# Who makes the low halves of the gate weights: VectorE takes over half 0 in the state-space stage of a two-block transformer kernel

## The chip, the cores and the metric

The kernel runs on one core of a Trainium2 chip. The metric is the device time of one execution in microseconds (us). Engines are named as the profile names them: PE (TensorE, the matrix multiplies), PEld (its weight loads), DVE (VectorE), ACT (ScalarE), POOL (GpSimd) and SP (SyncE, which here only issues the weight transfers).

## The reference

The program computes two blocks of two layers each over 256 positions of 1024 channels. The second block (`second_block`) has in each layer a mixer with a sparse attention and a state-space branch, then a gated feed-forward network. The change touches the state-space scan of that mixer, which runs twice, once in each layer:

```
L = exp(where(tril, A_cs[l] - A_cs[s], -inf))      # per head, 32 heads in 4 groups of 8
y = (C B^T * L) @ (x * dt)  + x * d_skip           # CB is shared by the 8 heads of a group
y = y * silu(z)                                    # the gate product
```

Beside it PE computes `h @ w_in` for the two gates of the mixer (`g_attn`, `g_ssd`), which needs 1024 x 2048 weights.

## The kernel before

All matrix products with weights go through slabs. A slab holds 1024 x 256 weights in two halves of 128 x 1024 numbers (128 partitions, 8 chunks of 128). SP loads a half into `w_raw`; ACT rounds it to `w_hi` (L1157, a type that PE multiplies at full rate); then DVE or POOL makes the remainder `w_lo = w_raw - w_hi` (L477, `split_lo`). PE multiplies each chunk three times (L675 to L677: high by high, low by high, high by low), 48 matmuls to a slab. `w_raw`, `w_hi` and `w_lo` have three buffers each. A remainder is made two slabs ahead of its use (`SPLIT_AHEAD`), a rounding three ahead. Each engine's program is written out by hand, and the engines wait for each other by semaphores. `s.w_lo[half]` counts the remainders of each half; when another engine goes on with a half, it first waits until the earlier owner's last remainder is counted (`take_over`).

The state-space stage works on pairs of heads, 16 pairs `c` to a layer, in groups of four that share one `cbm`. In this text "pair" always means a pair of heads. For each pair:

- PE writes the running sums of both heads into `logit` (L1088), and DVE takes differences of them (L2096, four instructions, `ssd_seg`).
- ACT takes the exponential of each head (L1530).
- DVE multiplies by `cbm` (L2104, 128x768, `ssd_m`), and PE multiplies by the inputs (L1122, eight matmuls into `tr` or `stat`).
- DVE adds the skip term (L2112, `ssd_out`, for the pair before), and POOL multiplies by the gate (L644, `ssd_gate`).

At the start of a group PE makes the group's `CB` (L1106, L1108) and DVE masks it (L2117, L2118). PE runs one slab of the gate weights ("gates") ahead of the products of every even pair. ACT rounds a later slab as soon as a slab is done, and after every odd slab it also takes one or two sigmoids (L1523), for which it loads another table and then the table of the exponential again. After the 16th pair DVE makes the last gate product itself (L2136), ACT squares (L1537), POOL adds the squares (L657), and DVE norms the groups (L2152, L2155, L486) beside the slabs of stage "pa"; the slabs of "ps" need the normed values.

Once in every two pairs, after an odd pair, DVE makes half 1 of the slab that is two ahead (`weights`, L1607 to L1610) right behind L2112, and POOL makes half 0 behind the gate products of the two pairs before. A gate product of an even pair and DVE's remainder wait for the same L2112, or follow it. Where this text says "inner piece" it means DVE's remainder behind the second pair of a group, and "end piece" the one behind the fourth, just ahead of the next L2117.

Of the kernel before, what the change touches and what calls it, by code (L numbers as in the profile page):

```python
# [19 lines left out]
ROUND_AHEAD, SPLIT_AHEAD = 3, 2  # L20
# [171 lines left out]
def build(nc, dram):  # L192
    ctx = ExitStack()
    with ctx:
# [269 lines left out]
        def slabs(stage, body, l=None):  # L464
            for n in range(COUNT[stage]):
                body(slab_at(stage, n, l), n, n % RING)
# [62 lines left out]
        @block.gpsimd  # L529
        def _(pool):  # L530
            def norm_lo(n, chunks):

                hi, lo = norm_set(n)
                for c in chunks:
                    pool.wait_ge(s.h_hi, DC * n + c + 1)
                    pool.wait_ge(s.h_f32, DC * n + c + 1)
                    lo_part(pool, lo[:, c, :], gained(n)[:, c, :], hi[:, c, :]).then_inc(s.h_lo_p, 1)

            def scaled_lo(layer):

                hi, lo = scaled_set(layer)
                for c in range(DC // 2):
                    pool.wait_ge(s.n_hi, DC * layer + c + 1)
                    pool.wait_ge(s.n_f32, DC * layer + c + 1)
                    lo_part(pool, lo[:, c, :], normed_f32(c), hi[:, c, :]).then_inc(s.n_lo_p, 1)

            def add_squares(n, j):

                pool.wait_ge(s.norm_sq, 4 * n + j + 1)
                if j == 2:  # L550
                    pool.wait_ge(s.norm_pre, 2 * n + 1)
                pool.tensor_tensor(sq[:, 0:2, :], sq[:, 0:2, :], sq[:, 2 * j:2 * j + 2, :], ALU.add).then_inc(s.norm_pre, 1)

            def residual(stage, n, l=None):

                for k in range(COUNT[stage]):
                    j = k - (COUNT[stage] - 4)
                    split_lo(pool, slab_at(stage, k, l).ahead(SPLIT_AHEAD), 0)
                    if j in (0, 1) and n < 8:
                        norm_lo(n, (2 * j, 2 * j + 1))  # L560
                    if j == 2:
                        add_squares(n, 1)
                        add_squares(n, 2)

            def opening(stage, layer, l=None):

                take_over(pool, stage, 1, l)
                for n in range(COUNT[stage]):
                    split_lo(pool, slab_at(stage, n, l).ahead(SPLIT_AHEAD), 0)
                    split_lo(pool, slab_at(stage, n, l).ahead(SPLIT_AHEAD), 1)  # L570
                    if n == 0:
                        scaled_lo(layer)

            def weights(stage, l=None, both=False):

                def body(slab, n, j):
                    split_lo(pool, slab.ahead(SPLIT_AHEAD), 0)
                    if both:
                        split_lo(pool, slab.ahead(SPLIT_AHEAD), 1)
                if both:  # L580
                    take_over(pool, stage, 1, l)
                slabs(stage, body, l)

            def ffn(f, n, l=None):

                sfx, base = stage_ffn(f, l)
                layer = n // 2 - 1

                def up(off):
                    def body(slab, n, j):  # L590
                        hi, lo = hid_parts(layer, n)
                        pool.wait_ge(s.hid_hi, base + off + n + 1)
                        lo_part(pool, lo, prod[:, j % 2:j % 2 + 1, :], hi).then_inc(s.hid_split, 1)
                    return body
                slabs("upA" + sfx, up(0), l)
                slabs("upB" + sfx, up(UP_A), l)
                take_over(pool, "dnB" + sfx, 0, l)
                residual("dnB" + sfx, n, l)

            nc.gpsimd.memset(eps[:, :], EPS)  # L600
            nc.gpsimd.memset(cum_parts[:, :].bitcast(F32), 0.0)
            nc.gpsimd.memset(ident_r[:, :].bitcast(F32), 0.0)
            nc.gpsimd.memset(u_pad[:, :, 0:CF_TAPS - 1], 0.0)
            nc.gpsimd.memset(t_pad[:, :, 0:SC_TAPS - 1], 0.0).then_inc(s.pads, 1)
            for b in range(2):
                nc.gpsimd.memset(prod[:, b, :], 0.0).then_inc(s.hid_split, 1)

            norm_lo(0, range(DC // 2))
            for n in range(SPLIT_AHEAD):
                split_lo(pool, Slab(s, n), 0)  # L610
            add_squares(0, 1)
            add_squares(0, 2)
            opening("ev_cf", 0)
            for stage in ("ev_sc", "ev_b"):
                weights(stage, both=True)
            residual("ev_out", 1)
            ffn(0, 2)
            opening("od_lru", 1)
            weights("od_qk", both=True)
            weights("od_v", both=True)  # L620
            residual("od_out", 3)
            ffn(1, 4)

            for l in range(2):
                opening("kidtwi", 2 + l, l)
                weights("qi", l, both=True)
                for stage in ("k", "q", "v", "xbc"):
                    weights(stage, l)
                for u in range(4):
                    split_lo(pool, slab_at("z", 2 * u, l).ahead(SPLIT_AHEAD), 0)  # L630
                    split_lo(pool, slab_at("z", 2 * u + 1, l).ahead(SPLIT_AHEAD), 0)

                    t, kv = u // 2, u % 2
                    out = (slice(None), slice(kv * QPK, (kv + 1) * QPK), slice(t * P, t * P + P))
                    raw = acc[:, u % 2, :, :].rearrange("p c (a b) -> p (c a) b", b=P)
                    pool.wait_ge(s.da_out, 4 * l + u + 1)
                    a_hi, a_lo = raw_set(2 + l)
                    pool.tensor_copy(a_hi[out], raw).then_inc(s.a_hi, 1)
                    pool.wait_ge(s.a_hi, 4 * l + u + 1)
                    lo_part(pool, a_lo[out], raw, a_hi[out]).then_inc(s.a_lo, 1)  # L640
                def ssd_gate(c, j):

                    pool.wait_ge(s.ssd_raw, XCH * l + c + 1)
                    pool.tensor_tensor(zs[:, c, :], y_raw[:, j % 2, :], zs[:, c, :], ALU.mult).then_inc(s.ssd_ydone, 1)  # L644

                def gates_weights(slab, n, j):
                    if n >= 1:
                        ssd_gate(2 * n - 1, 1)
                    ssd_gate(2 * n, 0)
                    split_lo(pool, slab.ahead(SPLIT_AHEAD), 0)  # L650
                slabs("gates", gates_weights, l)

                def bn_add(g):

                    pool.wait_ge(s.bn_sq, SG * l + g + 1)
                    at = 4 * (g % 2)
                    pool.tensor_tensor(sq[:, at:at + 2, :], sq[:, at:at + 2, :], sq[:, at + 2:at + 4, :], ALU.add)\  # L657
                        .then_inc(s.bn_pre, 1)

                bn_add(0)  # L660
                bn_add(1)
                for g in range(SG):
                    split_lo(pool, slab_at("pa", g, l).ahead(SPLIT_AHEAD), 0)
                    if g + 2 < SG:
                        bn_add(g + 2)
                weights("ps", l)
                residual("out", 5 + 2 * l, l)
                ffn(None, 6 + 2 * l, l)
# [913 lines left out]
        def _(dve):  # L1582
# [24 lines left out]
            def weights(slab, halves=(1,)):  # L1607

                for half in halves:
                    split_lo(dve, slab.ahead(SPLIT_AHEAD), half)  # L1610
# [307 lines left out]
            def layer(l):  # L1918
# [196 lines left out]
                def ssd_group(g, first):  # L2115
                    dve.wait_ge(s.ssd_cb, SG * l + g + 1)
                    tt(cbm[:, 0:T], tr[:, 0:T], const("tril", T + P)[:, 0:T], ALU.mult)  # L2117
                    tt(cbm[:, T:T + P], tr[:, T:T + P], const("tril", T + P)[:, T:], ALU.mult).then_inc(s.ssd_cbm, 1)  # L2118
                    dve.wait_ge(s.ssd_cbm, SG * l + g + 1)
                    for j in range(4):  # L2120
                        c = 4 * g + j
                        ssd_seg(c, j, 0)
                        ssd_seg(c, j, 1)
                        ssd_m(c, j)
                        if j >= 1 or not first:
                            ssd_out(c - 1, j + 3)
                        if j % 2:
                            weights(slab_at("gates", c // 2, l))
                ssd_group(0, True)
                for g in range(1, SG):  # L2130
                    ssd_group(g, False)
# [248 lines left out]
```

## Time and profile before

| | |
|---|---|
| time, median of 3 runs | 1809.47 us (1809.37 to 1809.75) |
| the profiled execution: its time, its span | 1810.56 us, 1808.7 us |
| busy: PE, DVE, ACT, POOL | 1731.5, 1362.1, 1020.6, 677.7 us |
| remainders L477 on POOL | 198, mean 2420 ns |
| remainders L477 on DVE | 348, mean 1426 ns |
| gate products L644 on POOL | 30, 736 to 1659 ns |
| the four groups of the first layer's stage begin at | 862.27, 880.12, 898.11, 916.61 us |
| the last gate product of that stage on DVE begins at | 935.43 us |

The span runs from the first to the last instruction; the profiled execution's time is 1.9 us longer than its span. Busy shares are means over a long program whose stages have different limits, so the stage is read by its own rows below.

### The profile page before, as it was taken

To read this page: it belongs to the slowest core of one execution; us is meant where nothing else is said; L and a number is where in the kernel's file an instruction comes from. 1 tells how busy PE (TensorE), PEld (TensorE's weight loads), DVE (VectorE), ACT (ScalarE), POOL (GpSimd) and SP (SyncE) were. 2 spreads that over 40 slices of the span, in tenths; PEclk is the share of its full clock that TensorE was granted. 3 is DMA by queue.
4 is the path that set the end of the run, shared out by engine and by line. 5 is a ranking of instruction groups with operands and counts; after the bars stand their busy time and mean duration, and the time that the engine had idled before them with its cause. 6 is when DMAs were issued, how large, how long until landed. Compare 5 with 4: busy or idle time off the path is not lost. (4 is left out here: it accounts for less than half of the span.)

```text
span 1808.7 us, 33606 instructions
## 1 busy us (share of the span) xinstructions
PE 1731.5 (96%) x13858; PEld 1686.1 (93%) x13858; DVE 1362.1 (75%) x1967; ACT 1020.6 (56%) x1571; POOL 677.7 (37%) x417
## 2 busy tenths in 40 slices
PE   6989999997999999999999999999999998999997
PEld 6989999986999999999889999999999888999997
DVE  5758875474686859994779589778997578769794
ACT  5465555673654564576663566546367565366462
POOL 6631104950310265344454501038334355331113
PEclk9999999998999999999999999999999999999999
DMA  7435645531455554454234455555354333545552
GB/s 268 151 112 180 201 166 176 195 114 35 146 188 185 168 189 152 163 182 143 99 125 164 163 174 196 178 176 186 129 176 163 117 116 130 176 152 196 187 173 85
DMA packets 80649, 288.42 MB, mean 159 GB/s; under 512 B 9072, under 2 KB 9328, under 8 KB 80368
## 3 DMA queue, kind: packets, MB, share of 16 engines
q1 hardware_dynamic: 79488, 283.15, 46.8%
q10 hardware_dynamic: 1008, 3.11, 0.5%
q8 instruction: 110, 1.80, 0.4%
q14 instruction: 43, 0.35, 0.1%
HBM read 285.18 MB, written 1.05 MB: 158 GB/s over the span
## 5 line engine op out<-in xcount | busy, mean ns | idle before, releaser
L1157 ACT ACTIVATE w_hi<-w_raw 128x1024 fp32r<-128x1024 f32 (+1 forms) x546 | 538.0, 1033 | 337.0 <-PE lin L677 336.0
L477 POOL TENSOR_TENSOR w_lo<-w_raw,w_hi 128x1024 fp32r<-128x1024 f32 (+1 forms) x198 | 476.9, 2420 | 360.9 <-ACT w_hi L1157 355.2
L675 PE MATMUL lin<-h_hi,w_hi 128*128 128x256 f32 x1952 | 560.6, 287 | 24.3 <-DVE w_lo L477 18.3
L675 PE MATMUL lin<-hid_hi,w_hi 128*128 128x256 f32 x1936 | 553.5, 286 | 10.5 <-DVE hid_lo L486 7.2
L676 PE MATMUL lin<-h_lo,w_hi 128*128 128x256 f32 x1952 | 555.3, 284 | 0.0
L677 PE MATMUL lin<-h_hi,w_lo 128*128 128x256 f32 x1952 | 555.2, 284 | 0.0
L676 PE MATMUL lin<-hid_lo,w_hi 128*128 128x256 f32 x1936 | 548.6, 283 | 0.0
L677 PE MATMUL lin<-hid_hi,w_lo 128*128 128x256 f32 x1936 | 548.5, 283 | 0.0
L477 DVE TENSOR_TENSOR w_lo<-w_raw,w_hi 128x1024 fp32r<-128x1024 f32 (+1 forms) x348 | 495.1, 1426 | 36.9 <-ACT w_hi L1157 35.9
L675 PEld LDWEIGHTS lin<-h_hi,w_hi 128*128 128x128 f32 x1952 | 377.7, 194 | 26.5 <-issue 17.5
L675 PEld LDWEIGHTS lin<-hid_hi,w_hi 128*128 128x128 f32 x1936 | 372.2, 192 | 13.3 <-DVE hid_lo L486 6.1
L676 PEld LDWEIGHTS lin<-h_lo,w_hi 128*128 128x128 f32 x1952 | 377.8, 194 | 0.8 <-issue 0.5
L677 PEld LDWEIGHTS lin<-h_hi,w_lo 128*128 128x128 f32 x1952 | 377.6, 193 | 0.0
L676 PEld LDWEIGHTS lin<-hid_lo,w_hi 128*128 128x128 f32 x1936 | 372.4, 192 | 0.3
L677 PEld LDWEIGHTS lin<-hid_hi,w_lo 128*128 128x128 f32 x1936 | 372.3, 192 | 0.0
L1691 DVE SCALAR_TENSOR_TENSOR acc<-arena,par,acc 128x254 f32<-128x254 f32 (+1 forms) x264 | 156.4, 632 | 3.0
L486 POOL TENSOR_TENSOR h_lo<-arena,h_hi 128x256 fp32r<-128x256 f32 x48 | 36.3, 764 | 279.5 <-ACT h_hi L1215 219.2
L486 POOL TENSOR_TENSOR hid_lo<-arena,hid_hi 128x256 fp32r<-128x256 f32 x48 | 36.3, 762 | 258.6 <-ACT hid_hi L1215 219.2
L1669 DVE TENSOR_TENSOR x<-x,lin 128x512 f32<-128x512 f32 x64 | 43.8, 685 | 100.8 <-PE lin L677 100.8
L1705 DVE TENSOR_TENSOR arena<-lin,std 128x512 f32<-128x512 f32 x88 | 60.7, 690 | 60.5 <-PE lin L677 60.3
L1227 ACT ACTIVATE acc<-arena,par 128x256 f32<-128x256 f32 x88 | 48.3, 596 | 93.8 <-DVE arena L1705 93.8
L1223 ACT ACTIVATE acc<-arena,par 128x256 f32<-128x256 f32 x44 | 26.5, 603 | 112.1 <-DVE arena L1705 112.1
(307 smaller groups left out, 2148.3 us busy)
## 6 DMA issues: line engine op xcount, KB each, us to landing
w_raw<-in_upA SPq DMA_DIRECT2D x112, 512.0 KB, 3.6
w_raw<-in_upB SPq DMA_DIRECT2D x64, 512.0 KB, 4.2
w_raw<-in_xbc SPq DMA_DIRECT2D x48, 512.0 KB, 4.1
w_raw<-in_dnA SPq DMA_DIRECT2D x32, 512.0 KB, 3.5
w_raw<-in_dnB SPq DMA_DIRECT2D x32, 512.0 KB, 3.4
w_raw<-in_z SPq DMA_DIRECT2D x32, 512.0 KB, 4.1
w_raw<-in_gates SPq DMA_DIRECT2D x32, 512.0 KB, 3.8
w_raw<-in_ps SPq DMA_DIRECT2D x32, 512.0 KB, 4.0
```

The source lines that it names most:

```text
L477: eng.tensor_tensor(w_lo[slab.slot][:, half, part], w_raw[slab.slot][:, half, part], w_hi[slab.slot][:, half, part].bitcast(F32), ALU.subt ...
L486: return eng.tensor_tensor(lo, whole, hi.bitcast(F32), ALU.subtract)
L675: nc.tensor.matmul(out, lhs[0], rhs[0], start=first, stop=False)
L676: nc.tensor.matmul(out, lhs[0], rhs[1], start=False, stop=False)
L677: return nc.tensor.matmul(out, lhs[1], rhs[0], start=False, stop=last)
L1157: nc.scalar.activation(w_hi[slab.slot][:, half, part], w_raw[slab.slot][:, half, part], ACT.Copy)\
L1223: nc.scalar.activation(acc[:, b, 0, :], zz[:, j, 0, :], ACT.Identity, bias=pcol(f"fb{f}", c), scale=pcol(f"fw{f}", 2 * FC + c)).then_inc(s ...
L1227: ins = nc.scalar.activation(acc[:, b, i, :], zz[:, j, i, :], ACT.Identity, bias=pcol2(l, "fb", i * FC + c), scale=pcol2(l, "fw", 2 * 2 * ...
L1669: tt(pairs[:, j, :, :], pairs[:, j, :, :], lin[slab.bank][:, :, :], ALU.add)\
L1691: ins = stt(outs[i][:, d:T], ins_[i][:, 0:T - d], weight(taps - 1 - d, i), outs[i][:, d:T], ALU.mult, ALU.add)
L1705: tt(zz[:, j, :, :], lin[slab.bank][:, :, :], std[:, 0, 0:T].unsqueeze(1).to_broadcast([P, 2, T]), ALU.mult).then_inc(s.bank_free[slab.ban ...
```

## The change

In the state-space stage POOL no longer makes remainders: its program there is gate products only. DVE makes both halves, half 0 and then half 1, at the place where it made half 1. Two waits hand the counter of half 0 over: DVE's ahead of the first group, and POOL's behind its last gate product.

```
@@ POOL
                     ssd_gate(2 * n, 0)
-                    split_lo(pool, slab.ahead(SPLIT_AHEAD), 0)
                 slabs("gates", gates_weights, l)
+                take_over(pool, "pa", 0, l)
@@ DVE
                         if j % 2:
-                            weights(slab_at("gates", c // 2, l))
+                            weights(slab_at("gates", c // 2, l), (0, 1))
+                take_over(dve, "gates", 0, l)
                 ssd_group(0, True)
```

DVE's order in the first group, from the skip term of the first pair on, before (`w_lo` is the remainder, `sq<-logit,dt_tok_sb` the differences of the running sums, `arena<-sq,arena` of L2104 the product with `cbm`):

```order
634 L2112 SCALAR_TENSOR_TENSOR sq<-arena,par,tr 128x256
635 L477 TENSOR_TENSOR w_lo<-w_raw,w_hi 128x1024
636 L2096 TENSOR_SCALAR sq<-logit,dt_tok_sb 128x256
637 L2096 TENSOR_SCALAR sq<-logit,dt_tok_sb 128x128
638 L2096 TENSOR_SCALAR sq<-logit,dt_tok_sb 128x256
639 L2096 TENSOR_SCALAR sq<-logit,dt_tok_sb 128x128
640 L2104 TENSOR_TENSOR arena<-sq,arena 128x768
```

And the same place in the changed kernel:

```order
634 L2112 SCALAR_TENSOR_TENSOR sq<-arena,par,tr 128x256
635 L477 TENSOR_TENSOR w_lo<-w_raw,w_hi 128x1024 x2
636 L2096 TENSOR_SCALAR sq<-logit,dt_tok_sb 128x256
637 L2096 TENSOR_SCALAR sq<-logit,dt_tok_sb 128x128
638 L2096 TENSOR_SCALAR sq<-logit,dt_tok_sb 128x256
639 L2096 TENSOR_SCALAR sq<-logit,dt_tok_sb 128x128
640 L2104 TENSOR_TENSOR arena<-sq,arena 128x768
```

One instruction has become two; the rest of DVE's order stands. The same happens at each of the eight places of a layer.

POOL's order in the state-space stage of the first layer, from its last attention work (L638, L486) to its additions of squares (L657); a minus is a row of before, a plus one of the change, and eight more rows with a minus of the same kind follow those shown:

```order
 L486 TENSOR_TENSOR h_lo<-acc,h_hi 128x4x128
-L644 TENSOR_TENSOR arena<-sq,arena 128x256
-L477 TENSOR_TENSOR w_lo1<-w_raw1,w_hi1 128x1024
-L644 TENSOR_TENSOR arena<-sq,arena 128x256 x2
-L477 TENSOR_TENSOR w_lo2<-w_raw2,w_hi2 128x1024
-L644 TENSOR_TENSOR arena<-sq,arena 128x256 x2
-L477 TENSOR_TENSOR w_lo0<-w_raw0,w_hi0 128x1024
-L644 TENSOR_TENSOR arena<-sq,arena 128x256 x2
...
+L644 TENSOR_TENSOR arena<-sq,arena 128x256 x15
 L657 TENSOR_TENSOR sq<-sq 128x512 x2
```

Eight remainders a layer have left POOL's queue, and its 15 gate products stand in one row.

## Rows read from the trace of the kernel before

**Rows 1.** Page, part 1: busy time and share of each engine, whole span

```profile
PE 1731.5 (96%) x13858; PEld 1686.1 (93%) x13858; DVE 1362.1 (75%) x1967; ACT 1020.6 (56%) x1571; POOL 677.7 (37%) x417
```

**Rows 2.** Windows: length, busy time by engine, PEclk, DMA share, GB/s

```profile
862.27:880.12 17.85, 17.14 (x142) 15.24 (x141) 14.06 (x27) 11.30 (x16) 6.19 (x4) 1.00 0.17 60
898.11:916.61 18.50, 17.24 (x142) 15.43 (x141) 14.46 (x28) 11.55 (x17) 9.51 (x7) 1.00 0.34 114
1430.86:1504.00 73.14, 68.72 (x564) 61.55 (x564) 57.80 (x113) 45.77 (x64) 35.05 (x23) 1.00 0.30 102
```

**Rows 3.** Waits: PE in 862.27 to 935.43, then in 940 to 990

```profile
PE stat L1122 <- DVE arena L2104: 4.4, 8, 0.9
...
PE lin L675 <- DVE hid_lo L486: 3.9, 1, 3.9
```

**Rows 4.** The chain that ended last, second layer's stage: start, us, what

```profile
1463.63 1.99 ACT w_hi L1157 x2
...
1469.33 0.95 ACT sq L1530 x2
...
1473.69 0.97 DVE arena L2104
...
1474.80 0.87 PE stat L1122 x8
```

**Rows 5.** Timeline of DVE: start, us, line, tiles, shapes [idle before <- releaser]

```profile
878.53 1.22 DVE L477 TENSOR_TENSOR w_lo<-w_raw,w_hi 128x1024 fp32r<-128x1024 f32 x1
880.12 0.42 DVE L2117 TENSOR_TENSOR arena<-tr,cst 128x256 f32<-128x256 f32 x1 [0.38 <-PE tr L1108]
883.32 0.96 DVE L2104 TENSOR_TENSOR arena<-sq,arena 128x768 f32<-128x768 f32 x1 [1.14 <-ACT sq L1530]
886.63 0.96 DVE L2104 TENSOR_TENSOR arena<-sq,arena 128x768 f32<-128x768 f32 x1 [0.66 <-ACT sq L1530]
887.90 1.22 DVE L477 TENSOR_TENSOR w_lo<-w_raw,w_hi 128x1024 fp32r<-128x1024 f32 x1
889.03 1.39 DVE L2096 TENSOR_SCALAR sq<-logit,dt_tok_sb 128x256 f32<-128x256 f32 x4
891.09 1.80 DVE L2104 TENSOR_TENSOR arena<-sq,arena 128x768 f32<-128x768 f32 x1 [0.66 <-ACT sq L1530]
901.80 0.96 DVE L2104 TENSOR_TENSOR arena<-sq,arena 128x768 f32<-128x768 f32 x1 [1.64 <-ACT sq L1530]
```

**Rows 6.** Timeline of POOL, the same columns

```profile
888.07 1.65 POOL L644 TENSOR_TENSOR arena<-sq,arena 128x256 f32<-128x256 f32 x1 [2.57 <-DVE sq L2112]
889.68 2.40 POOL L477 TENSOR_TENSOR w_lo<-w_raw,w_hi 128x1024 fp32r<-128x1024 f32 x1
893.37 0.74 POOL L644 TENSOR_TENSOR arena<-sq,arena 128x256 f32<-128x256 f32 x1 [1.29 <-DVE sq L2112]
```

**Rows 7.** Timelines of DVE and POOL at two starts of a "dnA" stage

```profile
214.83 2.90 DVE L477 TENSOR_TENSOR w_lo<-w_raw,w_hi 128x1024 fp32r<-128x1024 f32 x2
...
215.18 1.47 POOL L486 TENSOR_TENSOR hid_lo_far<-arena,hid_hi_far 128x256 fp32r<-128x256 f32 x1 [2.79 <-ACT hid_hi_far L1215]
...
1693.49 2.35 DVE L477 TENSOR_TENSOR w_lo<-w_raw,w_hi 128x1024 fp32r<-128x1024 f32 x2
...
1694.10 2.34 POOL L486 TENSOR_TENSOR hid_lo_far<-arena,hid_hi_far 128x256 fp32r<-128x256 f32 x1 [3.07 <-ACT hid_hi_far L1215]
```

**Rows 8.** Timelines of DVE and POOL behind the first layer's stage

```profile
935.43 2.54 DVE L2136 TENSOR_TENSOR arena<-sq,arena 128x256 f32<-128x256 f32 x1 [0.31 <-POOL arena L644]
...
946.00 4.10 DVE L2155 SCALAR_TENSOR_TENSOR arena<-arena,par,std 128x256 f32<-128x256 f32 x4
...
953.53 4.83 DVE L2155 SCALAR_TENSOR_TENSOR arena<-arena,par,std 128x256 f32<-128x256 f32 x4
...
970.16 1.67 DVE L2155 SCALAR_TENSOR_TENSOR arena<-arena,par,std 128x256 f32<-128x256 f32 x4
...
935.29 2.40 POOL L477 TENSOR_TENSOR w_lo<-w_raw,w_hi 128x1024 fp32r<-128x1024 f32 x1
```

More of the change, by code:

```diff
@@ L649, in gates_weights @@
                     ssd_gate(2 * n, 0)
-                    split_lo(pool, slab.ahead(SPLIT_AHEAD), 0)
                 slabs("gates", gates_weights, l)
+                take_over(pool, "pa", 0, l)
                 def bn_add(g):
@@ L2127, in ssd_group @@
                         if j % 2:
-                            weights(slab_at("gates", c // 2, l))
+                            weights(slab_at("gates", c // 2, l), (0, 1))
+                take_over(dve, "gates", 0, l)
                 ssd_group(0, True)
```

## The prediction

> **What bounds the kernel now.** I read four views, from the whole to the single instruction. The page first: PE is busy 96% of the span, DVE 75%, POOL 37% [rows 1]. That says that nearly every wait of PE costs time, and nothing yet on this stage. The windows next: in the state-space stage PE is busy 17.14 to 17.24 us of a group's 17.85 to 18.50, at full clock throughout (PEclk 1.00), so it idles 0.7 to 1.3 us a group, and DVE is busy 14.1 to 14.5 [rows 2]. PE's waits name the cause: 4.4 us in eight waits, all for L2104 on DVE [rows 3]. So whatever makes L2104 later makes PE later.
>
> The chain of waits shows which way round the loop the time goes [rows 4]. Slab done at 1463.63, then ACT's two roundings, its tables and sigmoids, exponentials at 1469.33, DVE's L2104 of the next pair at 1473.69, PE's products at 1474.80, and the next slab. DVE's remainders don't stand in this chain. The timeline of DVE tells how far off they are [rows 5]. Between its difference instructions and L2104 DVE always idles at least 0.66 us, ACT's latency. Ahead of a group's first L2104 it idles longer, 1.14 in the second group and 1.64 in the third (the fourth reads 1.63), because ACT is not yet through with its sigmoids. What lies over 0.66 is slack: 0.48, 0.98 and 0.97 us. The L2117 ahead of it waits another 0.38 us for PE: with the end piece at 878.53 and its successor 1.13 us behind it (887.90 to 889.03), DVE would be free at 879.66, and L2117 starts at 880.12, so the end piece has 0.46 us of its own. Inner pieces have no slack: the instructions behind them run back to back to an L2104 with the least idle of 0.66.
>
> **The change part by part.** *Removed:* 8 POOL remainders of 2.40 us a layer [rows 6]. POOL is not on the path. But one at 889.68 runs to 892.08, and the L2104 that starts at 891.09 takes 1.80 instead of 0.96 us and ends 0.81 behind POOL's [rows 5, 6]: it waited for POOL. One L2104 in four is slow in this way, the one behind an inner piece. The change gives back 0.84 us at each.
>
> *Added:* a second DVE remainder right behind the first. By itself it costs 1.13 us of DVE, start to start. How it fares depends on POOL's gate product, which still comes 0.17 us behind the start of the first (887.90, 888.07). There the product took 1.65 us instead of the 0.74 of one that meets nothing, and ended 0.69 us after DVE had gone on to its next instruction at 889.03 [rows 5, 6]. So it waited for DVE's remainder to end. Now another remainder stands where it used to get through. The trace has four places with two DVE remainders in a row and a POOL operation of the same 128x256 size that starts during the first, the first at 214.83, the last at 1693.49, and they disagree [rows 7]. In two, POOL got in between: the pair took 2.90 us. In the other two POOL waited for both: the pair took 2.35 and POOL 2.34. The difference is 0.55 us. So a pair costs 1.13 us more than one remainder if POOL waits, and 1.13 + 0.55 = 1.68 if it gets in between. I take 1.68: where POOL asked earliest, 0.35 us behind the first remainder's start (214.83 to 215.18), it got in, and here it asks at 0.17.
>
> The Trainium skill has the rule behind this (SBUF — State Buffer, "Who interferes with whom"): a VectorE instruction with two SBUF inputs and a GpSimd instruction that reads SBUF exclude each other, and the one issued first keeps the ports for its whole length. The slow L2104 and the slow gate product agree with it. By it the gate product, issued ahead of the second remainder, would always go first, which is the 1.68; the places where POOL waited for both speak against it, and by those the cost would be 1.13.
>
> *The sum,* as the shift of a group's first L2104 and what follows, with POOL in between. An inner piece adds 1.68 - 0.84 = 0.84, an end piece 1.68 less its slack.
> - Second group: 0.84 + 1.68 - 0.46 - 0.48 = 1.58.
> - Third group: 0.84 + 1.68 - 0.46 - 0.98 = 1.08 more, 2.66. (ACT itself is late by only the 1.58, so DVE decides.)
> - Fourth: 0.84 + 1.68 - 0.46 - 0.97 = 1.09 more, 3.75.
> - Its inner piece: 4.59 at the last L2104, so at PE's last products and at the first slab of "pa".
>
> The end of the stage: DVE's last skip term and L2136 are behind the fourth end piece, 4.59 + 1.68 = 6.3 us later. L2136 gets back what POOL's remainder of 935.29 cost it (2.54 us, against some 0.42 that I estimate from L2117 of the same 128x256) and its 0.31 wait: 6.3 - 2.1 - 0.3 = 3.9, under the 4.59 of PE. So ACT's next rounding and root, which wait for PE's slab too, shift by 4.59, and so does the norm chain; PE's 3.9 us wait for it behind "pa" [rows 3] moves with it and doesn't absorb it. The four groups of the second layer repeat the first (73.14 us against 935.43 - 862.27 = 73.16) [rows 2]. Two layers: 9.2 us. Against the profiled execution 1810.56 + 9.2 = 1819.8; against the median, 1.1 lower, **1818.7 us**, 0.5% slower.
>
> *At nothing:* the two waits of the handover. The remainders they wait for were made in time: POOL's last of stage "z" ended before DVE's first group, and POOL's next job behind its wait, adding squares, waits for ACT's squares anyhow, which come behind L2136. POOL's lighter queue gives nothing, since its gate products are waited for only at L2136. The transfers into `w_raw` half 0 can start some 3 us sooner (DVE's first would end at 889.12, POOL's ended at 892.08); no row has a wait on a transfer here. No buffer is freed later than PE needs it: remainders are two slabs ahead of their use.
>
> **The rivals.**
> 1. *POOL waits for both.* An inner piece adds 1.13 - 0.84 = 0.29. Second group: 0.29 + 1.13 - 0.94 = 0.48. Then 0.29 + 1.13 - 1.44 is nothing, and ACT's own 0.48 stays the floor. With the last inner piece 0.77 a layer: 1809.47 + 1.5 = 1811.0. For it: two of four places. Against: the early request.
> 2. *POOL gets in at some pieces only.* If at inner ones alone: 0.84 + 1.13 - 0.94 = 1.03, then 0.53 and 0.54 more and 0.84, 2.94 a layer: 1815.4. If at end ones alone: 0.29 + 1.68 - 0.94 = 1.03, 0.53, 0.54 and 0.29, 2.39 a layer: 1814.3.
> 3. *Faster: the norms behind the stage come free of POOL.* Two groups of L2155 take 4.10 and 4.83 us there against 1.67 undisturbed [rows 8], held up by POOL's "pa" remainders. If POOL, no longer coming from a remainder, runs ahead of them, up to 2.43 + 3.16 = 5.6 us a layer come back: with rival 1's cost 1811.0 - 11.2 = 1799.8. It decides from 5.2 us of gain on, nearly half. Against: these remainders follow additions that wait for ACT's squares and roots, which move with the norms.
> 4. *PE's longer waits lower the clock.* They grow from 0.9 at most to about 1.2 us. The stage shows PEclk 1.00 with the 0.9 ones. If 6 us of each layer ran at half clock, a length that I choose, no row has one in this stage, 3 us a layer more: 1824.7.
>
> **How the numbers follow.** Forecast (POOL always or nearly always in between) 0.60; rival 2 0.13; rival 1 0.18; rival 3 0.05; rival 4 or another added wait 0.04. A measurement of this kernel tells about 0.2% from no change, 3.6 us. Faster by more: 0.05. Within: rival 1, 0.18. Slower by more: 0.77. The range leaves out rivals 3 and 4 and reaches from just under rival 1, 1810.6, to 2.8 us over the forecast, 1821.5, half of rival 4's price. The forecast's own range is 1816.5 to 1821.
>
> **What would show it.** DVE's pairs of L477 take 2.90 us and gate products between them end 0.7 us after the second's start (right), or 2.35 with gate products of about 2.8 us (rival 1). No L2104 over 1 us. Groups begin 19.6 to 19.9 us apart (18.0 to 18.8 in rival 1); PE's waits for L2104 near 9 us a layer. L2136 about 0.4 us. L2155 still near 4.1 and 4.8 (else rival 3). The prediction is wrong if DVE idles ahead of a group's first L2104 stay over 0.66 us, since then ACT and not DVE sets the pace.

## The result

The changed kernel takes 1817.36 us (median of 6 runs, 1814.81 to 1818.89) against 1809.45 us (1809.13 to 1809.75). The ratio is 1.0043, 95% interval 1.0033 to 1.0053: 7.9 us slower. Forecast were 1818.7 us and a range of 1810.6 to 1821.5.

The page of the profile after, part 1 (compare rows 1):

```profile
PE 1728.9 (95%) x13858; PEld 1684.3 (93%) x13858; DVE 1374.4 (76%) x1983; ACT 1020.7 (56%) x1571; POOL 640.4 (35%) x401
```

DVE has 16 instructions more and POOL 16 fewer, and both differ less than the 16 remainders alone would make. Windows of the first and third group in the first layer, and of the whole stage up to the last gate product (columns as in rows 2):

```profile
858.71:878.59 19.88, 18.33 (x151) 16.43 (x151) 16.50 (x30) 12.47 (x18) 4.04 (x3) 1.00 0.18 60
898.13:917.66 19.53, 17.22 (x142) 15.40 (x141) 16.85 (x31) 11.63 (x17) 4.77 (x4) 1.00 0.34 108
858.71:937.71 79.00, 70.08 (x575) 62.92 (x575) 67.56 (x121) 47.00 (x65) 18.34 (x15) 1.00 0.30 98
```

A group took 17.85 and 18.50 us in [rows 2] and takes 19.88 and 19.53. The stage up to L2136's start is 79.00 us long, where it was 935.43 - 862.27 = 73.16. In the third group DVE is busy 16.85 of 19.53 us. Nearly all of the rest are its four idles of 0.66 us ahead of L2104, the latency of the exponentials. PE stands at full clock. PE's waits in this stage, and behind it:

```profile
PE stat L1122 <- DVE arena L2104: 8.9, 8, 1.6
...
PE lin L675 <- DVE hid_lo L486: 3.9, 1, 3.9
```

The eight waits for L2104 have doubled from 4.4 us [rows 3]; the one behind stage "pa" is as long as it was, so it took nothing up.

The timeline of DVE after, at the same places as rows 5:

```profile
875.77 2.89 DVE L477 TENSOR_TENSOR w_lo<-w_raw,w_hi 128x1024 fp32r<-128x1024 f32 x2
878.58 0.41 DVE L2117 TENSOR_TENSOR arena<-tr,cst 128x256 f32<-128x256 f32 x1
881.28 0.96 DVE L2104 TENSOR_TENSOR arena<-sq,arena 128x768 f32<-128x768 f32 x1 [0.66 <-ACT sq L1530]
...
885.87 2.90 DVE L477 TENSOR_TENSOR w_lo<-w_raw,w_hi 128x1024 fp32r<-128x1024 f32 x2
...
890.72 0.96 DVE L2104 TENSOR_TENSOR arena<-sq,arena 128x768 f32<-128x768 f32 x1 [0.66 <-ACT sq L1530]
```

And POOL's gate products (compare rows 6):

```profile
886.03 1.65 POOL L644 TENSOR_TENSOR arena<-sq,arena 128x256 f32<-128x256 f32 x1 [2.58 <-DVE sq L2112]
...
892.15 0.73 POOL L644 TENSOR_TENSOR arena<-sq,arena 128x256 f32<-128x256 f32 x1 [4.48 <-DVE sq L2112]
```

Four things are to be seen. The pairs of remainders take 2.89 and 2.90 us, all 16 of them. The gate product that asks during the first ends at 887.68, 0.68 us behind the start of the second: it got in between. L2117 waits for nothing now, and the idle ahead of a group's first L2104 is down to 0.66 us, so the slack of 0.46, 0.48, 0.98 and 0.97 us is used up. And L2104 behind an inner piece takes 0.96 us and not 1.80: the refund is there.

Times in different kernels are compared here from the start of the stage, the first L2117 of a layer, since the work ahead of it varies from run to run: it begins at 862.27 us in the profile before and at 858.71 after, with the same instructions ahead of it. (So the two profiled executions, 1810.56 and 1814.81 us, are only 4.3 us apart; the second is the shortest of its six.) So far from the start of the stage, the changed kernel is later than the one before by 1.52 us at the end of the second group's first L2104, 2.58 in the third group, 3.63 in the fourth, 4.44 at the last L2104 of a layer, and 3.83 at the end of the last norm remainder (L486). The two layers agree within 0.03 us. Twice 3.83 is 7.7 of the 7.9 us between the medians.

### The profile page after: what moved, and what is told of

It is laid out like the page before. It is cut to its first block, busy times and chain, and to the rows that moved or that the text cites. A ratio compares the mean times of both kernels' runs of the same rounds, so it can differ in the third digit from the quotient of the medians.

```text
span 1813.0 us, 33608 instructions
## 1 busy us (share of the span) xinstructions
PE 1728.9 (95%) x13858; PEld 1684.3 (93%) x13858; DVE 1374.4 (76%) x1983; ACT 1020.7 (56%) x1571; POOL 640.4 (35%) x401
## 4 chain that ended last, share of the span: by engine, by line
PE 69%; DVE 23%; ACT 4%; issue 3%; DMA 0%; POOL 0%; SPq 0%; DVEq 0%; ACTq 0%
PE lin L675 21%; PE lin L677 21%; PE lin L676 21%; DVE w_lo L477 5%; DVE acc L1691 3%; DVE sq L2096 2%; DVE arena L2156 1%; ACT w_hi L1157 1%; DVE arena L1982 1%; ACT sq L1530 1%; PE stat L748 1%; DVE stat L1933 1%; PE tr L851 1%; DVE arena L1992 1%; DVE sq L2112 1%
## 5 line engine op out<-in xcount | busy, mean ns | idle before, releaser
L477 POOL TENSOR_TENSOR w_lo<-w_raw,w_hi 128x1024 fp32r<-128x1024 f32 (+1 forms) x182 | 438.4, 2421 | 358.7 <-ACT w_hi L1157 353.0
L477 DVE TENSOR_TENSOR w_lo<-w_raw,w_hi 128x1024 fp32r<-128x1024 f32 (+1 forms) x364 | 519.6, 1435 | 37.5 <-ACT w_hi L1157 36.5
L486 POOL TENSOR_TENSOR h_lo<-arena,h_hi 128x256 fp32r<-128x256 f32 x48 | 36.2, 761 | 279.4 <-ACT h_hi L1215 219.3
L486 POOL TENSOR_TENSOR hid_lo<-arena,hid_hi 128x256 fp32r<-128x256 f32 x48 | 36.2, 762 | 256.8 <-ACT hid_hi L1215 219.2
```

The costliest lines, as they stand in the source:

```text
L477: eng.tensor_tensor(w_lo[slab.slot][:, half, part], w_raw[slab.slot][:, half, part], w_hi[slab.slot][:, half, part].bitcast(F32), ALU.subt ...
L486: return eng.tensor_tensor(lo, whole, hi.bitcast(F32), ALU.subtract)
```

## The experiments

The table gives the shift against the kernel before of a layer's second group's first L2104, of its last L2104, and of the end of the norms behind the stage (mean of both layers), then the difference of the median times and the 95% interval of the ratio. The experiments ran beside the kernel before, whose median was 1809.21 to 1809.33 us there. The code pieces below are shortened: definitions, unchanged lines and some waits that hand a counter over are left out.

| kernel | first L2104, group 2 | last L2104 | norms | time | ratio |
|---|---|---|---|---|---|
| changed kernel | +1.52 | +4.44 | +3.83 | +7.9 | 1.0033 to 1.0053 |
| e1_gate_late | +0.43 | +1.23 | +0.62 | +2.1 | 1.0004 to 1.0022 |
| e2_end_only | +0.71 | +1.15 | +0.55 | +2.6 | 1.0004 to 1.0021 |
| e3_inner_only | +0.82 | +3.25 | +3.30 | +6.8 | 1.0026 to 1.0051 |
| e4_column_only | -0.31 | -1.61 | -2.21 | -2.8 | 0.9975 to 0.9992 |
| e5_two_parts | -0.31 | -1.61 | -1.11 | -1.0 | 0.9985 to 1.0003 |
| e6_ask_later | +1.51 | +4.41 | +3.80 | +8.4 | 1.0035 to 1.0062 |
| e7_ask_latest | +1.50 | +4.41 | +3.82 | +8.4 | 1.0031 to 1.0059 |
| e8_spread | +1.37 | +7.0 | +7.3 | +15.0 | 1.0072 to 1.0100 |
| e9_parts_last_dve | -0.30 | -1.60 | -1.86 | -2.7 | 0.9976 to 0.9994 |

**e1: the gate product can't get in between.**

```
@@ POOL, changed kernel
+                    pool.wait_ge(s.w_lo[1], slab.number + SPLIT_AHEAD + 1)
                     ssd_gate(2 * n, 0)
```

> The changed kernel, but POOL's gate product of an even pair also waits until both remainders behind it on DVE are made, so it can't get in between them. Theory (the 0.55 us that the product takes from each of 16 pairs is a good part of the loss, and slack takes up most of the rest): pairs take 2.35 us, gate products 0.74, the groups begin 18.8, 18.0 and 18.5 us apart, the last L2104 of a layer is 0.8 us later than in the kernel before instead of 4.5, and the time is 1811.0 us (1810.3 to 1812). Rival (the loss is the remainder's own time on DVE, the product in between only comes along): 16 pairs less 0.55 us save nothing that counts, the time stays at 1816 to 1818. Rival (POOL's later products become a wait of their own): DVE waits at L2112 or L2136 and the time is over 1813.

Measured: 1811.39 us. DVE and POOL in the second group of e1:

```profile
888.90 2.35 DVE L477 TENSOR_TENSOR w_lo<-w_raw,w_hi 128x1024 fp32r<-128x1024 f32 x2
...
891.33 0.73 POOL L644 TENSOR_TENSOR arena<-sq,arena 128x256 f32<-128x256 f32 x1 [4.84 <-DVE w_lo L477]
```

DVE makes exactly the same 16 remainders more than before, and 5.8 of the 7.9 us are gone. So the product in between is what made the change expensive: 16 times 0.55 us, which end pieces can't hide either, since they stand above their slack with it. The rival that DVE's added work is the loss by itself falls. The first group is 18.78 us long, as expected; the last L2104 is 1.23 us late where 0.8 was expected, which e3 explains.

**e2 and e3: one half of the change each.** In e2 DVE makes both halves behind the fourth pair of a group, in e3 behind the second; at the other place POOL makes half 0 as before.

```
@@ POOL, kernel before; e2 (in e3 != 0)
                     ssd_gate(2 * n, 0)
-                    split_lo(pool, slab.ahead(SPLIT_AHEAD), 0)
+                    if n % 2 != 1:
+                        pool.wait_ge(s.w_lo[0], slab.number + SPLIT_AHEAD)
+                        split_lo(pool, slab.ahead(SPLIT_AHEAD), 0)
@@ DVE (in e3 == 0)
+                            if c // 2 % 2 == 1:
+                                take = slab_at("gates", c // 2, l)
+                                dve.wait_ge(s.w_lo[0], take.number + SPLIT_AHEAD)
+                                weights(take, (0, 1))
+                            else:
+                                weights(slab_at("gates", c // 2, l))
```

> DVE makes both halves only behind the fourth pair of each group; behind the second POOL makes half 0 as before. Theory (an end piece costs 1.68 us less the slack of 0.46 + 0.48, then 0.46 + 0.98): the groups' first L2104 shift by 0.74, 0.98 and 1.23 us, the last one of a layer by 1.23, in all 2.5 us: 1811.9 (1811.2 to 1812.7). One L2104 in four stays at 1.8 us. Rival (no slack, each of the 16 pieces costs the same half microsecond): half of the loss, 3.9 us, 1813.4.

Measured: 1811.82 us, where 1811.9 was expected. The shifts of a group's first L2104 are 0.71, 0.93 and 1.16 us (expected 0.74, 0.98, 1.23). The slack of the end pieces is as read. That the time itself is so near is partly luck: behind the norms only 0.55 us a layer are left of 1.15, and 1.5 us of the difference in time stand outside stage and norms (see the end of the next section). The waits added for handing the counter to and fro show no cost in the shifts.

> DVE makes both halves only behind the second pair of each group; behind the fourth POOL makes half 0 as before. Theory (an inner piece costs 1.68 - 0.84 = 0.84 us; where slack is left at the group's start, 0.48 and 0.98, it takes this up): the first L2104 of the second group shifts by 0.36 us and the later ones no further, the last of a layer by 1.2, in all 2.4 us: 1811.9 (1811.2 to 1812.7). So the two halves of the change cost 4.9 us alone and some 8 together. Rival (each piece the same): 3.9 us, 1813.4. Rival (inner pieces have no slack anywhere): 4 x 0.84 a layer, 6.7 us, 1816.2.

Measured: 1816.07 us. This falls on the rival "no slack anywhere" (1816.2), not on the theory. The first L2104 of groups 2 to 4 shifts by 0.82, 1.63 and 2.44 us: each inner piece's 0.82 us goes on in full. I had let the slack ahead of the next group take it up, with ACT unmoved. ACT isn't unmoved. Timeline of ACT in e3, behind an inner piece:

```profile
894.59 1.18 ACT L1533 ACTIVATE sq<-sq 128x384 f32<-128x384 f32 x2 [2.14 <-DVE sq L2099]
895.67 1.99 ACT L1160 ACTIVATE w_hi<-w_raw 128x1024 fp32r<-128x1024 f32 x2
897.68 1.28 ACT L1526 ACT_TABLE_LOAD   x1
```

The roundings start right behind the exponentials of the fourth pair, without idle, and these wait for DVE. What is late at an inner piece makes these exponentials late, then the roundings, the sigmoids, and the next group's exponentials. It is so in the kernel before too:

```profile
893.97 1.17 ACT L1530 ACTIVATE sq<-sq 128x384 f32<-128x384 f32 x2 [2.99 <-DVE sq L2096]
895.05 1.99 ACT L1157 ACTIVATE w_hi<-w_raw 128x1024 fp32r<-128x1024 f32 x2
```

The chain of waits had named PE's slab as what releases the roundings [rows 4], and I followed only that. The slab's last matmul had ended some 0.3 us before them; ACT itself was not free earlier.

**e4: POOL's remainders left out.** POOL makes one column of 1024, so this kernel leaves most of half 0's low parts out of its result.

```
@@ POOL, kernel before
-                    split_lo(pool, slab.ahead(SPLIT_AHEAD), 0)
+                    pool.tensor_tensor(w_lo[...][:, 0, 0:1], w_raw[...][:, 0, 0:1], w_hi[...][:, 0, 0:1], ALU.subtract)
```

> The kernel before, with POOL's remainders of the state-space stage cut to one column of 128x1 (so half 0 of the gate weights' low parts is mostly left out of the computation): what the removal of POOL's remainders gives by itself. Theory: no L2104 takes more than 0.96 us, but the groups still begin 17.9, 18.0 and 18.5 us apart, since ACT sets their pace, and only the last inner piece's 0.84 us counts, 0.77 of it before PE stops waiting: 1809.45 - 1.5 = 1807.9 (1807.2 to 1808.6). Rival (each of the four 0.84 us of a layer counts): 6.7 us, 1802.7. Rival (none counts, ACT's squares set the end): 1809.4.

Measured: 1806.42 us, a little under the expected 1807.2 to 1808.6. The groups are 17.36, 17.77 and 18.28 us long: with L2104 back at 0.96 us each group gains 0.2 to 0.5 us and not nothing, for the reason that e3 gives, and the last inner piece gives 0.87 more. It is not the full 0.84 a group, since the roundings behind a fourth pair now idle 0.45 to 0.55 us until PE's slab is done. So POOL's remainders cost some 2.8 us where they stand in the kernel before, which bounds what moving them could give.

**e5: POOL's remainders moved out of L2104's way.** `part_lo` makes a part of a remainder's columns, and `to` is the slab two ahead.

```
@@ POOL, kernel before
                     if n >= 1:
                         ssd_gate(2 * n - 1, 1)
+                        if n % 2:
+                            part_lo(slab.ahead(SPLIT_AHEAD - 1), slice(HALF // 2, HALF)).then_inc(s.w_lo[0], 1)
                     ssd_gate(2 * n, 0)
-                    split_lo(pool, slab.ahead(SPLIT_AHEAD), 0)
+                    if n % 2 == 0:
+                        to.wait_hi(pool, 0)
+                        part_lo(to, slice(0, HALF // 2))
+                    else:
+                        if n == COUNT["gates"] - 1:
+                            pool.wait_ge(s.ssd_ydone, XCH * (l + 1))
+                        split_lo(pool, to, 0)
```

> The kernel before (POOL makes half 0), but placed so that POOL's remainders don't meet DVE's two-input instructions: behind the second pair of a group POOL makes the first 512 columns ahead of the next gate product and the other 512 behind it, and the last remainder of a layer waits for L2136. Theory (what costs in the kernel before is POOL holding up one L2104 in four, by 0.84 us, and what the end of the stage loses to POOL's last remainder): no L2104 over 1.1 us, group starts at 17.4, 35.1 and 53.5 us as in e4, L2136 at 0.42 us, and 1806.6 us (1805.6 to 1807.6), under both kernels. Rival (the second part, asked for near 893.2 and 1.2 us long, still meets the next L2104, or the first part meets this one): two L2104 a group at 1.2 to 1.8 us and no gain, 1809 to 1811.

Measured: 1808.33 us, not to be told from the kernel before. POOL and DVE in the second group (L647 is a part, L2117 of this kernel the product that is L2104 elsewhere), then POOL at the end of the stage:

```profile
889.97 1.30 POOL L647 TENSOR_TENSOR w_lo<-w_raw,w_hi 128x512 fp32r<-128x512 f32 x1
892.81 0.74 POOL L644 TENSOR_TENSOR arena<-sq,arena 128x256 f32<-128x256 f32 x1 [1.54 <-DVE sq L2125]
893.51 1.29 POOL L647 TENSOR_TENSOR w_lo<-w_raw,w_hi 128x512 fp32r<-128x512 f32 x1
...
891.38 0.96 DVE L2117 TENSOR_TENSOR arena<-sq,arena 128x768 f32<-128x768 f32 x1 [0.66 <-ACT sq L1543]
...
894.70 0.96 DVE L2117 TENSOR_TENSOR arena<-sq,arena 128x768 f32<-128x768 f32 x1 [0.66 <-ACT sq L1543]
...
935.36 3.32 POOL L477 TENSOR_TENSOR w_lo<-w_raw,w_hi 128x1024 fp32r<-128x1024 f32 x1 [0.61 <-DVE arena L2149]
938.64 2.52 POOL L670 TENSOR_TENSOR sq<-sq 128x512 f32<-128x512 f32 x2
```

The stage is now e4's to 0.01 us, with the whole computation in it: the parts fit ahead of and behind both L2104. But the last remainder, behind L2136, meets DVE's own remainder there and takes 3.32 us, and the additions of squares start at 938.64. That is 75.76 us behind the start of the stage, where e4's start at 74.22 and those of the kernel before at 76.87. Of 1.61 us won 1.11 are left behind the norms, where e4 kept 2.21. The time is the least certain one here: the four executions with a granted clock of 0.988 took 1806.07 to 1806.88 us, the seven at 0.985 and 0.986 took 1807.74 to 1809.71.

**e6 and e7: the product asks later.**

```
@@ POOL, changed kernel; e7 has 0:256 (`late` is a scratch buffer)
+                    pool.wait_ge(s.ssd_raw, XCH * l + 2 * n + 1)
+                    nc.gpsimd.memset(late[:, 0:32], 0.0)
                     ssd_gate(2 * n, 0)
```

> The changed kernel with a memset of 128x32 on POOL ahead of the gate product of each even pair, so that the product asks later within DVE's first remainder (0.2 to 0.4 us behind its start instead of 0.16). Theory (whoever asks first goes first, so any product that asks before the first remainder ends gets in between): pairs still take 2.90 us, the time stays at the changed kernel's 1817. Rival (only an early product gets in): pairs take 2.35 us, 1811.4.

> The same with a memset of 128x256, so that the product asks some 0.5 to 0.7 us behind the first remainder's start, as at the four places of the kernel before where one got in at 0.35, one at 0.61 and two at 0.61 had to wait. Theory (asked first goes first): 2.90 us and 1817. Rival (past some point near 0.6 us the second remainder is ahead in the queue): pairs of 2.35 us with gate products of over 2 us, 1811.4.

Measured: 1817.75 and 1817.73 us. DVE and POOL in e7:

```profile
888.97 2.90 DVE L478 TENSOR_TENSOR w_lo<-w_raw,w_hi 128x1024 fp32r<-128x1024 f32 x2
...
889.11 0.31 POOL L651 MEMSET late<- 128x256 f32 x1 [2.56 <-DVE sq L2115]
889.38 1.41 POOL L645 TENSOR_TENSOR arena<-sq,arena 128x256 f32<-128x256 f32 x1
```

The product now asks 0.22 us (e6) and 0.41 us (e7) behind the first remainder's start, in e7 less than the 0.5 to 0.7 us aimed at, and gets in between each of 32 times. So from 0.16 to 0.41 us it makes no difference when it asks. Why two of the four places of the kernel before went the other way at 0.61 us [rows 7] these runs don't tell. It isn't chance: in all 11 traces of this case the first two places go POOL's way (asked at 0.35 and 0.61 us) and the last two DVE's (0.61).

**e8: the two remainders apart.**

```
@@ DVE, changed kernel
-                        if j % 2:
-                            weights(slab_at("gates", c // 2, l), (0, 1))
+                        weights(slab_at("gates", c // 2, l), (j % 2,))
```

> The changed kernel, but with DVE's two remainders apart: half 0 behind each even pair, half 1 behind each odd one. No gate product can get between two remainders, so the 16 x 0.55 us are gone, and DVE's work is the same. Theory (where a remainder stands counts, and only the place ahead of a group's start has slack): a remainder behind the first or the third pair of a group adds its full 1.13 us, the refund of 0.84 is once a group, so each group is 1.42 us later than before, 5.7 us at the last L2104 of a layer against the changed kernel's 4.4, less 0.6 us at the end of the stage: 1819.5 (1818 to 1820.5). Rival (the port alone makes the loss): 1811 to 1812.

Measured: 1824.37 us, the slowest, and nearly 5 us over the theory. The first group is 19.23 us long, 1.38 over the kernel before as expected (1.42), the second of the first layer 19.40, 1.40 over. Then the clock comes in: the third, in which it falls, is 20.64 us long, 2.14 over. Windows in e8's first layer, every 20 us:

```profile
881.00:901.00 20.00, 17.83 (x147) 16.01 (x146) 16.47 (x33) 11.62 (x18) 6.58 (x4) 1.00 0.35 115
901.00:921.00 20.00, 17.95 (x137) 15.72 (x136) 15.31 (x29) 10.81 (x15) 6.57 (x4) 0.91 0.29 97
921.00:941.00 20.00, 17.77 (x128) 15.91 (x128) 14.20 (x28) 9.49 (x15) 4.99 (x4) 0.83 0.31 104
```

And e8's waits of PE from 901 to 941:

```profile
PE stat L1122 <- DVE arena L2104: 4.3, 2, 2.2
```

PEclk falls to 0.91 and 0.83, so part of those stretches ran at the lower of the two levels, 1.2 GHz, with two waits of up to 2.2 us in them; the changed kernel, whose waits are 1.6 us at most, shows 1.00 throughout the stage. But the longest wait alone doesn't decide. In e8's second layer the clock stood at 1.00 up to 1464.9 us, and fell then, when no wait of that stage had been longer than this one:

```profile
1463.90 0.87 PE L1122 MATMUL stat<-arena 128*64 128x256 f32 x8 [1.57 <-DVE arena L2104]
```

```profile
1455.00:1475.00 20.00, 18.43 (x141) 16.60 (x140) 15.95 (x30) 10.75 (x16) 6.39 (x5) 0.91 0.32 106
```

The port is free of pairs here, all L2104 take 0.96 us, and the kernel is slower by 7 us than the changed one, and by 13 than e1, which makes the same remainders with no product in between either: where DVE's work stands counts as much as how much there is. How much of it is the place and how much the clock is an estimate: by the theory the place alone would have given 1819.5.

**e9: e5 with the last remainder on DVE.**

```
@@ POOL, e5
+                    if n == COUNT["gates"] - 1:
+                        pool.wait_ge(s.w_lo[1], to.number + 1)
                     ssd_gate(2 * n, 0)
...
-                    else:
-                        if n == COUNT["gates"] - 1:
-                            pool.wait_ge(s.ssd_ydone, XCH * (l + 1))
-                        split_lo(pool, to, 0)
+                    elif n < COUNT["gates"] - 1:
+                        split_lo(pool, to, 0)
@@ DVE
+                            if c == XCH - 1:
...
+                                weights(take, (0, 1))
```

> e5 (POOL's remainders in the inner pieces cut in two round a gate product), but the last remainder of half 0 of a layer is made by DVE behind half 1, with the gate product beside it asked for behind both; POOL makes none there. In e5 that last one stood behind L2136 and made POOL's additions of squares 1 us late, so that only 1.1 of the 1.6 us won at the last L2104 were left behind the norms. Theory: the stage as in e5 (the last L2104 1.6 us sooner than before), L2136 at 0.42 us, and 2.2 us a layer left behind the norms as in e4: 1806 (1805 to 1807.3), under both kernels. Rival (DVE's 1.13 us more ahead of L2136 reach ACT's squares): no more left than in e5, 1808.3.

Measured: 1806.54 us, 2.7 us under the kernel before, and 10.8 under the changed one by the medians. The intervals of e5 and e9 overlap; that e9 is the better is told by the norms, 1.86 us a layer ahead of the kernel before and not 1.11. Here the change is made in the one place where it pays: DVE has both halves behind the 16th pair, the product asks behind both, and POOL's additions of squares begin 75.02 us behind the start of the stage (862.36 us in e9), 0.74 sooner than in e5:

```profile
932.43 2.35 DVE L477 TENSOR_TENSOR w_lo<-w_raw,w_hi 128x1024 fp32r<-128x1024 f32 x2
...
935.71 0.43 DVE L2155 TENSOR_TENSOR arena<-sq,arena 128x256 f32<-128x256 f32 x1 [0.53 <-POOL arena L644]
...
934.87 0.74 POOL L644 TENSOR_TENSOR arena<-sq,arena 128x256 f32<-128x256 f32 x1 [4.04 <-DVE w_lo L477]
937.38 2.54 POOL L671 TENSOR_TENSOR sq<-sq 128x512 f32<-128x512 f32 x2 [1.77 <-ACT sq L1551]
```

## Why the prediction was right, point by point

- *The price of a pair* (1.68 us over one remainder, with the product in between): right. All 16 pairs take 2.90 us, and e1 shows what the 0.55 us is worth by taking only it away: 5.8 us of 7.9. The choice between the two ends was made on one place of four and was confirmed here at 0.16, 0.22 and 0.41 us; the rule of the Trainium skill cited there (SBUF — State Buffer, "Who interferes with whom") agrees at every one of these 48 products, and still not at two of the four places.
- *The refund* (0.84 us at each inner piece): right, 1.80 to 0.96 us, and e4 shows it alone.
- *The slack of the end pieces:* right. It is all used (L2117 without a wait, idle 0.66 us), and e2 gives 0.71, 0.93 and 1.16 us for 0.74, 0.98 and 1.23.
- *The sum in the stage:* 1.58, 2.66, 3.75 and 4.59 us forecast, 1.52, 2.58, 3.63 and 4.44 measured.
- *"ACT itself is late by only the 1.58, so DVE decides":* the reason was wrong and the number stood. ACT is late by the inner piece too, by the exponentials of the fourth pair (e3). In the changed kernel that is 1.52 + 0.82 = 2.34, and DVE's own 2.58 is still more. With inner pieces alone it decides, and my figure for e3 was too low by 4.2 us. Rival 1 and the mixed rival had the same mistake: e1 came to 1.23 us at the last L2104, not 0.77.
- *The end of the stage:* the one term that was mis-sized. I let all of the 4.59 us pass to the norms, because ACT's rounding and root would "wait for PE's slab too". 4.44 us come to the last L2104 and 3.83 leave the norms, 0.6 less in each layer. L2136 takes 0.42 us, as expected, where it took 2.54. What it gives back was not lost behind PE, as I had it: before, ACT's rounding stood behind its squares and a sigmoid, which wait for L2136, and had no idle; now it waits for PE. So the first reciprocal (L2152) shifts by 4.24 and not 4.43 us. Before (first row) and after:

```profile
940.39 2.00 ACT L1157 ACTIVATE w_hi<-w_raw 128x1024 fp32r<-128x1024 f32 x2
```

```profile
941.06 2.01 ACT L1157 ACTIVATE w_hi<-w_raw 128x1024 fp32r<-128x1024 f32 x2 [0.41 <-PE lin L677]
```

And of DVE's norm work the third group of L2155 is shorter. Before (first row) and after:

```profile
962.93 2.67 DVE L2155 SCALAR_TENSOR_TENSOR arena<-arena,par,std 128x256 f32<-128x256 f32 x4
```

```profile
946.68 4.11 DVE L2156 SCALAR_TENSOR_TENSOR arena<-arena,par,std 128x256 f32<-128x256 f32 x4
...
954.22 4.83 DVE L2156 SCALAR_TENSOR_TENSOR arena<-arena,par,std 128x256 f32<-128x256 f32 x4
...
963.62 2.24 DVE L2156 SCALAR_TENSOR_TENSOR arena<-arena,par,std 128x256 f32<-128x256 f32 x4
```

Rival 3's two large ones stay at 4.1 and 4.8, as forecast, but the third gives back 0.43 us. e1 and e2, where POOL also has no remainder at the end of the stage, lose the same 0.6 us between the last L2104 and the norms, e3, where it has one, loses nothing. That the missing remainder is the reason is shown by these. The steps stand in the traces. Before, PE waited for POOL's additions of squares:

```profile
940.50 1.13 PE L1130 MATMUL tr<-sq,cst 128*128 128x256 f32 x4 [0.34 <-POOL sq L657]
```

After, L1130 runs without that wait, so PE's slabs behind it come 3.83 us later and not 4.43, and with them ACT's roundings and POOL's "pa" remainders. The one beside the third L2155 starts 0.17 us behind DVE's third reciprocal, where it started 0.60 behind it, and the third L2155 is held up less by that difference. Other runs have other distances, and the length of the third L2155 follows: 0.17, 0.52, 0.60, 0.67 and 0.89 us go with 2.24 (e4), 2.58 (e9), 2.67 (before), 2.73 (e3) and 2.95 us (e5). 0.6 and the 0.15 of the stage, in two layers, are the 1.5 us between 9.2 and 7.7.
- *PE's waits:* forecast near 9 us and no lower clock: 8.9 us, PEclk 1.00. The longest is 1.6, not 1.2 us. That waits for L2104 can bring the lower clock, rival 4's mechanism, e8 shows, with waits of 1.57 to 2.2 us ahead of it; in the changed kernel they did not.

In e1, e2, e4, e5 and e9 the difference in time is 0.9 to 1.6 us more than twice the shift of the norms. It is within the intervals of the ratios, which are some 3 us wide, but it has one sign throughout, and the granted clock on record fits it: its mean over the executions is 0.9863 to 0.9866 in these five against 0.9874 to 0.9876 for the kernel before beside them. A clock lower by 0.001 means 3.6 us more of the 1809 at half clock, at most 1.8 us of work. In e3, whose clock is lower by 0.0003 alone, 0.2 us are left over. Why these kernels run a little longer at the lower clock no run tells.

## What to carry to other kernels

Before work moves from one engine to another, look whether the two contend for something, and then ask who asks first: two operations in a row on the engine that matters leave a gap where the other engine's waiting operation slips in, and here that gap, not the moved work, made most of the loss. Read slack at each place where the work would stand; 1.13 us cost nothing behind the last pair of the later groups (e1) and all of 1.13 behind a first or third pair (e8). And follow every input of the instruction that sets the pace: the chain of waits named what the instruction waits for, but its own engine had come free later, and with that the time went another way.

## What the runs showed of the hardware

- A POOL operation that has asked for its turn during a first DVE instruction with two SBUF inputs goes ahead of a second such instruction right behind it: 16 of 16 in the changed kernel, 32 of 32 in e6 and e7, at a price of 0.54 us for the second (1.76 instead of 1.22). At two of four other places, asked at 0.61 us, POOL waited for both instructions (2.34 us) in all 11 traces, which no run explains.
- A remainder of 128x512 takes POOL 1.29 to 1.30 us, of 128x1024 2.40: cutting it in two costs 0.2 us and made it fit between two DVE products.
- Waits of PE of up to 1.6 us left the granted clock at 1.00 in the changed kernel's stage; in e8 it fell to 0.91 and 0.83 over 20 us stretches, with waits of up to 2.2 us in the first layer, but in the second behind one of 1.57 us. So the longest wait alone doesn't tell whether it falls.
